# Two pairs of retention scores and two products with V at other slots of each layer's schedule

## The reference, cut to what matters

```python
for l in range(DEPTH_2):
    h = _rmsnorm(x, norm_mix[l])
    z = h @ w_in[l]
    ...
    o_nsa = _nsa(q_n, kc, vc, ks, vs, kw, vw, g_n, ...)    # 8 heads: compressed, selected and window attention
    o_ret = _retention(q_r, k_r, v_r, g_r, ret_gn[l])      # 4 heads
    o_conv = _conv_module(c_a, c_b, ...)                   # 31 taps along the tokens
    ...
    # in _nsa, per head:    s = q.k + bias;  p = softmax(s);  o = p @ v
    # in _retention:        inner = einsum('bnchd,bnehd->bnhce', qc, kc) * decay;  o_inner = inner @ v
```

## Time and profile before

| | |
|---|---|
| median of 3 runs | 1150.87 us (1149.76 to 1150.96) |
| the profiled execution | 1151.39 us |
| its span, first to last instruction | 1149.5 us |
| mean granted clock of TensorE | 0.998 |
| TensorE matmul busy | 1136.5 us, 99% |
| TensorE weight load busy | 950.7 us, 83% |
| VectorE busy | 823.6 us, 72% |
| ScalarE busy | 586.6 us, 51% |
| GpSimd busy | 137.2 us, 12% |

### The profile page before, as it was taken

One profiled execution on the slowest core, in us unless ns is written; L12 is line 12 of the kernel. 1 busy time (PEld: TensorE's weight loads), 2 busy tenths in 40 slices (PEclk: granted clock), 3 DMA queues, 4 the chain that ended last, 5 costly groups with the idle time before them and its releaser, 6 DMA issues.

```text
span 1149.5 us, 15956 instructions
## 1 busy us (share of the span) xinstructions
PE 1136.5 (99%) x6207; PEld 950.7 (83%) x6207; DVE 823.6 (72%) x1245; ACT 586.6 (51%) x736; POOL 137.2 (12%) x152
## 2 busy tenths in 40 slices
PE   7999999999999999999999999999999999999997
PEld 6888777788998777888888888998777888888886
DVE  5565657647689899787777454699899787777443
ACT  7445575644426666634555333525776544455332
POOL 1222231200003143100000000003234000000000
PEclk9999999999999999999999999999999999999999
DMA  9546553457545777654555555545678554555641
GB/s 361 198 168 206 188 199 112 167 189 293 179 151 198 209 184 220 192 191 166 195 195 195 202 190 191 178 152 216 188 210 225 184 182 156 212 184 189 222 157 37
DMA packets 35323, 219.34 MB, mean 191 GB/s; under 512 B 3888, under 2 KB 5680, under 8 KB 10928
## 3 DMA queue, kind: packets, MB, share of 16 engines
q1 hardware_dynamic: 32800, 204.67, 50.9%
q0 software_dynamic: 1728, 12.58, 5.9%
q10 hardware_dynamic: 720, 1.06, 0.3%
HBM read 217.25 MB, written 1.05 MB: 190 GB/s over the span
## 4 chain that ended last, share of the span: by engine, by line
PE 83%; issue 15%; ACT 1%; POOL 0%; DMA 0%; DVE 0%; POOLq 0%; ACTq 0%; DVEq 0%
PE panel L947 33%; PE panel L951 16%; PE panel L1018 5%; PE panel L921 5%; PE tile L1032 4%; PE panel L1021 3%; PE panel L995 3%; PE panel L994 3%; PE panel L993 3%; PE heads_out L1382 1%; PE heads_out L1235 1%; PE tile L1296 1%; PE tile L1405 1%; PE tile L1402 1%; DMA area<-in_x_columns_dram 0%
## 5 line engine op out<-in xcount | busy, mean ns | idle before, releaser
L630 DVE TENSOR_TENSOR ring_parts<-ring,ring_parts 128x2048 fp32r<-128x2048 f32 (+2 forms) x172 | 390.0, 2271 | 160.6 <-ACT ring_parts L596 154.7
L596 ACT ACTIVATE ring_parts<-ring 128x2048 fp32r<-128x2048 f32 (+2 forms) x184 | 346.9, 1888 | 253.5 <-PE panel L951 187.8
L947 PE MATMUL panel<-ring_parts,hT 128*128 128x512 f32 (+2 forms) x1184 | 289.7, 391 | 2.5 <-issue 2.5
L947 PEld LDWEIGHTS panel<-ring_parts,hT 128*128 128x128 f32 x1184 | 211.7, 189 | 49.8 <-issue 9.9
L947 PE MATMUL panel<-ring_parts,area_parts 128*128 128x512 f32 x736 | 177.4, 389 | 0.0
L947 PEld LDWEIGHTS panel<-ring_parts,area_parts 128*128 128x128 f32 x736 | 137.9, 188 | 28.5
L951 PE MATMUL panel<-ring_parts,hT 128*128 128x512 f32 (+2 forms) x592 | 149.2, 387 | 0.0
L1018 PE MATMUL panel<-hT,ring_parts 128*128 128x512 f32 x512 | 129.9, 393 | 0.0
L951 PEld LDWEIGHTS panel<-ring_parts,hT 128*128 128x128 f32 x592 | 106.5, 188 | 22.7 <-issue 2.5
L2244 DVE SCALAR_TENSOR_TENSOR area<-area,cw 128x256 f32<-128x256 f32 x240 | 104.7, 497 | 2.9
L1018 PEld LDWEIGHTS panel<-hT,ring_parts 128*128 128x128 f32 x512 | 91.6, 189 | 15.9
(11 more groups left out here) (250 smaller groups left out, 1231.6 us busy)
## 6 DMA issues: line engine op xcount, KB each, us to landing
ring<-in_w_layers_dram SPq DMA_DIRECT2D x140, 1024.0 KB, 4.9
ring<-in_w_first_dram SPq DMA_DIRECT2D x38, 1024.0 KB, 5.0
ring_parts<-in_w_layers_dram POOLq DMA_DIRECT2D x12, 1024.0 KB, 8.8
ring<-in_w_first_dram SPq DMA_DIRECT2D x5, 512.0 KB, 9.9
area<-in_second_bias_dram SPq DMA_DIRECT2D x8, 320.0 KB, 3.1
ring<-in_w_layers_dram SPq DMA_DIRECT2D x4, 560.0 KB, 4.0
area<-in_first_bias_dram SPq DMA_DIRECT2D x4, 384.0 KB, 4.4
area<-in_later_bias_dram SPq DMA_DIRECT2D x1, 1536.0 KB, 12.0
```

What stands on the lines that cost most here:

```text
L596: act.activation(ring_lo[:, SLOTS + hi, 0:w], ring[:, slot, 0:w], ACT.Copy).then_inc(high_ready, 1)
L630: g.tensor_tensor(ring_lo[:, slot, 0:w], ring[:, slot, 0:w], ring_lo[:, SLOTS + hi, 0:w], ALU.subtract).then_inc(low_ready, 1)
L947: pe.matmul(ps[:, b, 0:width], t[:, 4 * i + k, b * P:(b + 1) * P], hi[:, k, :], start=(i == k == 0 and t is of[0]), stop=False)
```

## The change

The retention scores `R0` go from slot 19 to slot 20 and `R2` from slot 21 to slot 22. The products with V of pairs 4 and 5 go from slots 40 and 43 to slots 36 and 44. By the order within a slot, slot 19 is then T4, T5, cmpS; slot 20 R0; slot 21 cmpN; slot 22 V of pair 2, then R2; slot 36 V of pair 4, then S of pair 6; slot 44 V of pair 5, then S of pair 7. `TAPS_AT` is not changed.

```diff
 LAYER_T = (6, 12, 19, 26, 31, 41, 47, 54)
-LAYER_V = (8, 15, 22, 29, 40, 43, 51, 55)
+LAYER_V = (8, 15, 22, 29, 36, 44, 51, 55)
 LAYER_SUM, LAYER_HIGH = (29, 57), (30, 61)
-LAYER_OTHER = dict(cmpHk=5, cmpFk=8, ro0=11, ro1=6, cmpHv=12, cmpFv=14, rot=17, cmp2=17, cmpS=19, cmpN=21, PcT=23, R0=19, R2=21, Or0=33, Or1=30, oR=48, cv=58, cz=62)
+LAYER_OTHER = dict(cmpHk=5, cmpFk=8, ro0=11, ro1=6, cmpHv=12, cmpFv=14, rot=17, cmp2=17, cmpS=19, cmpN=21, PcT=23, R0=20, R2=22, Or0=33, Or1=30, oR=48, cv=58, cz=62)
```

## The result

| | before | changed |
|---|---|---|
| median (runs) | 1150.14 us (5) | 1157.51 us (5) |
| lowest to highest | 1149.76 to 1150.96 | 1156.68 to 1160.78 |
| ratio, 95% interval | | 1.0064, 1.0053 to 1.0076 |
| profiled execution, its span | 1151.39, 1149.5 | 1157.61, 1155.8 |
| mean granted clock of it | 0.998 | 0.994 |

What follows compares the result with a forecast made beforehand. It took TensorE's own sum of pieces as the bound. Per layer 3.3 us delay less 0.5 saved made 5.6 for two layers, plus 2.8 for the clock: 8.4 us, 1159.3 us, range 1155.5 to 1161.5.

Steps and rivals of the forecast that it cites:

- The wait: At pair 4's scores, TensorE waits 3.5 us per layer for head 2's tile, held by two VectorE taps.
- The step: Slot 21's taps: GpSimd's scaling of pair 3 stays inside them, so eight instructions take 4.62 us.
- the prediction's own signs: At pair 4's scores: no wait means (c), under 2.5 us (b), a clock of 1.00 right behind it (a).
- (b): Rival at slot 21's taps: GpSimd does not slow them, pause 2.3 us, clock probably kept; 1154.1 us, chance 0.1.
- The rival with undisturbed taps: The same as (b): slot 21's taps not slowed by GpSimd, 2.1 us of delay per layer; 1154.1 us, chance 0.1.
- (a): Rival behind the wait at pair 4's scores: the wait comes but the clock holds; 1156.5 us, chance 0.2.
- R0 at nothing: Moving R0 to slot 20 costs TensorE nothing, between -0.05 and +0.05 us, and makes VectorE 0.3 us later.
- The products with V: At slots 36 and 44, each moved product saves one return to wide products, 0.5 us per layer together.
- (c): Rival for the whole layer: not slower, as the wait is given back later or is absent; 1149.4 us, chance 0.1.
- The clock: Behind the wait at pair 4's scores, the granted clock falls in both layers, 1.4 us each, 2.8 us together.
- Given back: The same as (c): a pause at pair 4 only brings forward a later one; 1149.4 us, chance 0.1.

Runs made afterwards that it cites:

- r2_only: The kernel before with only the second retention scores R2 moved, from slot 21 to slot 22; 1157.15 us in one run.
- r0_only: The kernel before with only the retention scores R0 moved, from slot 19 to slot 20; 1152.33 us in one run.
- only_r: The changed kernel with the products with V of pairs 4 and 5 back at slots 40 and 43; 1158.04 us.
- best_try: The kernel before with both V moves, R2 at slot 22 with slot 21's two taps behind it, and slot 38's tap at slot 44; 1151.62 us.
- taps_behind: The changed kernel with the two taps of slot 21 moved to slot 22, behind the decay of heads 2 and 3; 1151.43 us.
- v_relieved: The kernel before with both products with V moved as in the change and one tap moved from slot 38 to slot 44; 1150.68 us.
- taps_at_24: The changed kernel with the two taps of slot 21 moved to slot 24 and the tap of slot 38 moved to slot 44; 1151.67 us.
- only_v: The kernel before with only the products with V of pairs 4 and 5 moved, to slots 36 and 44; 1150.44 us.
- one_tap_each: The changed kernel with one of slot 21's two taps moved to slot 22, behind the decay; 1151.81 us.
- three_taps_ahead: The changed kernel with three taps instead of two in slot 21 and one instead of two in slot 25; 1164.56 us.

## Why the prediction was right, and where its numbers were off

**The wait, right in place and cause, too large.** Forecast: TensorE stands 3.5 us, pair 4 is 3.3 later. Measured: 2.6 and 13.06 - 10.47 = 2.59. The term that was mis-sized is the one of the eight taps, taken at 4.62 us; they took 3.41, 1.21 less. The step said that ScalarE's exponentials, and so GpSimd's scaling, "stays at its time and inside the taps". But GpSimd's three small instructions took 0.66 us longer, start to start, and the scaling began as the last tap ended. Three smaller errors went the other way. R0's later scores delay VectorE by 0.55 us up to the start of the taps (404.41 - 395.67 = 8.74 after the compressed scores, where the decay of head 2 in their place stood at 403.47 - 395.28 = 8.19), not by 0.3: the return behind the compressed scores was left out (0.11), and the decay waits for the whole of the second piece, line 1349, and not for half of it (0.11). r2_only, without R0's move, has its taps at 403.78 - 395.59 = 8.19. Between the taps and the decay lie 0.14 us (407.82 to 407.96), not 0.08. And from the start of the decay of head 2 to the scores it is 0.77 us (407.96 to 408.73), not 0.61. Together 3.3 - 1.21 + 0.25 + 0.06 + 0.16 = 2.56, against 2.59. By the prediction's own signs the wait is the forecast's only by a hair: under 2.5 us would have meant rival (b), and without R0's larger delay it would have been that. So the place and the cause were foreseen, and the size between the two was luck.

**The rival with undisturbed taps** put its time too low, though its condition came true. It took 2.1 us and a clock that probably holds. Pair 4 was 0.5 us later than that and the clock fell once. That the measured time lies nearer to the forecast than to (b) is owed to these, and to a range that reached down past (a).

**R0 at nothing, wrong.** "That the compressed scores stand in front of it saves nothing that the rows show" compared the scores' own 0.63 us. The saving is behind them, 0.11 us of return to wide products, and through VectorE the move costs 0.57 in all (r0_only). Together with R2's move it costs as much, as a part of the big wait: only_r, which has both, is 61.17 - 60.63 = 0.54 us over r2_only in layer 1, where the clock held in both.

**The products with V, right on TensorE and not enough of a price by itself.** Predicted 0.5 us per layer, measured 0.53 to 0.56 once VectorE is relieved, 0.38 in the changed kernel, 0 alone. The prediction asked whether VectorE has a step at a product with V, and it has none; but rival (c) had noted that VectorE runs without gaps in these panels, and the saving was not held against that. In the changed kernel 0.16 of it goes elsewhere: eight wide products from slot 46 on take 1.97 us, where 1.81 is usual, as PEld waits for the low parts there. The chain of the changed kernel, layer 0, shows the saving itself and that leak:

```profile
436.57 0.58 PE heads_out L1382 x4
437.15 0.22 PE heads_out L1386 x4
437.37 0.42 PE tile L1402 x4
437.79 0.43 PE tile L1405 x4
438.22 2.49 PE panel L947 x10
...
454.15 1.97 PE panel L951 x8
```

V and scores stand side by side, with one return behind them and none between, as the first block had it.

**The clock, right once in two.** Forecast two falls of 1.4 us each. The profile has one, of 6.70 - 5.11 = 1.59, of a wait that was shorter than forecast, and none in layer 1. The sum has it fall in both layers and rival (a) in neither; that one layer falls and the other, behind a wait as long, doesn't was in no case of the prediction. That the medians differ by 7.4 us and the profiled pair by 6.2 is mostly the kernel before, whose profiled run is 1.25 us above its own median. How often each layer falls can't be read from whole runs, as those of the kernel before scatter as widely.

**"Given back", out.** Nothing of the wait comes back later in the layer: in only_r, where the clock held, pair 4 is 2.59 us late and the stretch is 2.57 and 2.59 us longer.

So of the 8.4 us in the sum, the wait was 1.4 too much for two layers (3.3 against 2.6 each), the V moves 0.2 too good, and the clock 2.8 where one fall took 1.6: 8.4 - 1.4 + 0.2 - 1.2 = 6.0, and the profiled stretches grew by 5.92. The 7.4 us by the medians look nearer to 8.4 than that only because the kernel before had a lower median beside the changed kernel (1150.14) than beside the others (1151.28 and more).

## What to carry to other kernels

- Before a product is moved behind a tile's use, ask who empties that tile, and what stands ahead of the emptying on that engine. One slot on TensorE was worth 0.21 us (best_try's scores of pair 4 against those of the kernel before); the same slot crossed two taps on VectorE, and pair 4 was 2.05 us late by it (r2_only), ten times that.
- That no wait is listed doesn't say that there is slack. When TensorE was made 0.5 us shorter, a wait for VectorE took all of it back, at a place that the waits of the kernel before don't name. Look for the second chain (from TensorE's rare reads of the other engine's results back along that engine) and cost a saving at what that chain leaves.
- A price that depends on what two engines do at once (4.62 against 3.41 us here) is a pair of prices. When anything ahead of it shifts, take both ends.

## What the runs showed of the hardware

**Whether the clock falls isn't told by the length of the pause.** The chain of the changed kernel, first block, and its granted clock (the third number from the end):

```profile
27.06 1.88 issue
28.93 5.51 PE panel L947 x16
...
30.00:31.00 1.00, 1.00 (x4) 0.71 (x4) 1.00 (x1) 0.00 (x0) 0.00 (x0) 0.50 1.02 426
```

and of taps_behind, the same place:

```profile
26.20 2.65 issue
28.85 3.92 PE panel L947 x16
...
30.00:31.00 1.00, 1.00 (x6) 0.80 (x5) 1.00 (x1) 0.00 (x0) 0.00 (x0) 1.00 0.98 410
```

A pause of 1.88 us is followed by products at a granted clock of 0.50, one of 2.65 by products at 1.00. (They take 3.92 us there, and 3.90 behind v_relieved's pause of 1.38, both at 1.00; 3.63 is usual elsewhere.) At this place pauses of 2.12 to 2.55 us had the clock fall too (only_r, r2_only, taps_at_24, best_try and the kernel before), and pauses of 2.63 and 2.68 (only_v, one_tap_each) and of 1.75 (three_taps_ahead) had not. In the layers the waits of 2.6 us had it fall in one layer of the changed kernel and in neither of only_r, and those of 2.2 us in layer 0 of r2_only alone. Behind both waits of 5.4 us it was down; three_taps_ahead, layers 0 and 1:

```profile
413.00:414.00 1.00, 1.00 (x4) 0.81 (x3) 0.91 (x6) 1.00 (x3) 0.00 (x0) 0.50 0.00 0
...
846.00:847.00 1.00, 1.00 (x7) 0.35 (x4) 0.00 (x0) 0.00 (x0) 0.00 (x0) 0.50 1.10 467
```

From pair 4's scores to pair 5's this kernel takes 10.26 and 9.41 us where 7.61 is usual, so a fall cost 2.65 and 1.80 there, and 1.59 in the changed kernel. A pause of about 2 to 2.6 us in this kernel may cost some 1.5 us more than its length, or nothing. What decides between the two stays open.

**VectorE and GpSimd hold each other.** The instructions of taps with line 740 beside them take 4.62 us for eight (3.41 without), 6.21 for twelve (5.1), 2.80 for four (1.67): each time 1.1 to 1.2 us more, of the scaling's 1.5, and whatever their number. GpSimd is held as well: in layer 1 of taps_at_24 the same scaling takes 3.34 us where 1.47 is the least, beside a low part (line 630) that VectorE takes from 844.51 to 846.80.

```profile
844.79 3.34 POOL L740 TENSOR_TENSOR area<-area,stat 128x768 f32<-128x768 f32 x1
```

The decays, which read one of their two inputs from a tile in PSUM, keep their 0.42 and 0.28 us with the scaling beside them (407.96 and 408.30 in the changed kernel). The Trainium skill (SBUF — State Buffer, Who interferes with whom) says that a VectorE instruction with two SBUF inputs contends with a GpSimd instruction that reads SBUF, and one with at most one SBUF input doesn't. The trace agrees in both: the taps have two and pay once for the one GpSimd instruction, the decays have one and keep their time.
